# One encoder kernel with split-precision experts: which engine subtracts the low halves of the expert weights

## The reference

```python
def expert_choice_moe(h, w_router, w_gate_up, w_down):       # 16 experts, D = D_EXPERT = 1024
    aff = jax.nn.softmax((xt @ w_router).astype(jnp.float32), axis=-1)
    gate, idx = lax.top_k(aff.T, cap)                         # cap = 32 and 64 tokens: 96 for both sequences
    xs = xt[idx]
    gu = jnp.einsum('ecd,edf->ecf', xs, w_gate_up)            # 1024 x 2048 weights per expert
    g, u = gu[..., :D_EXPERT], gu[..., D_EXPERT:]
    y = jnp.einsum('ecf,efd->ecd', jax.nn.silu(g) * u, w_down) * gate[..., None]   # 1024 x 1024 per expert
    out = jnp.zeros_like(xt).at[idx.reshape(-1)].add(y.reshape(-1, D))
```

## Time and profile before

| | |
|---|---|
| three runs, median | 4184.73 us (4175.05 to 4191.94) |
| profiled execution, span from first to last instruction | 4180.8 us; its page gives no other time for it, and the span stands 3.9 us below the median of the runs |
| PE, PE weight loads | 3603.7 us (86%), 2737.9 us (65%) |
| DVE, ACT, POOL | 1949.1 us (47%), 1800.1 us (43%), 1069.5 us (26%) |
| first use of an expert's low half by PE, last scatter: layer 1 | 1395.8 us to 2087.8 us |
| last scatter, layer 2 | 4162.5 us |
| POOL low halves (L644) | 128 instructions, 612.6 us |
| DVE low halves (L1022) | 256 instructions, 878.8 us |

### The profile page before, as it was taken

One profiled execution on the slowest core, in us unless ns is written; L12 is line 12 of the kernel. 1 busy time (PEld: TensorE's weight loads), 2 busy tenths in 40 slices (PEclk: granted clock), 3 DMA queues, 4 the chain that ended last, 5 costly groups with the idle time before them and its releaser, 6 DMA issues.

```text
span 4180.8 us, 54944 instructions
## 1 busy us (share of the span) xinstructions
PE 3603.7 (86%) x19108; PEld 2737.9 (65%) x19108; DVE 1949.1 (47%) x2474; ACT 1800.1 (43%) x2780; POOL 1069.5 (26%) x604
## 2 busy tenths in 40 slices
PE   5999878899999688888869998788999987888886
PEld 4835645599998455556567375456999975556554
DVE  3423346222222777776734333452222237777775
ACT  3344445311112566666533444443111135666664
POOL 0021112100000556566500201111000005666664
PEclk9988988799999799999989899788999988999998
DMA  4101000211114689989641011002111227899896
GB/s 170 43 12 34 25 18 12 87 59 58 54 45 156 213 300 305 319 304 309 235 145 33 12 39 33 4 16 94 55 51 58 97 99 256 294 318 315 303 312 219
DMA packets 317901, 575.80 MB, mean 138 GB/s; under 512 B 14656, under 2 KB 100672, under 8 KB 317664
## 3 DMA queue, kind: packets, MB, share of 16 engines
q1 hardware_dynamic: 310288, 544.85, 37.2%
q0 software_dynamic: 7472, 29.17, 3.3%
HBM read 539.37 MB, written 40.89 MB: 139 GB/s over the span
## 4 chain that ended last, share of the span: by engine, by line
PE 70%; issue 12%; DVE 8%; POOL 6%; ACT 2%; DVEq 1%; DMA 1%; SPq 1%; POOLq 0%; ACTq 0%
PE bank L1413 13%; PE bank L1415 13%; PE bank L1414 13%; PE bank L1620 7%; PE bank L1471 5%; PE bank L1504 5%; PE bank L1641 4%; POOL wlo_more L644 4%; PE bank L1479 3%; PE bank L1499 2%; DVE wlo_more L1022 1%; PE bank L1574 1%; POOL PR L639 1%; PE bank L1576 1%; DVE YS L1400 1%
## 5 line engine op out<-in xcount | busy, mean ns | idle before, releaser
L1413 PE MATMUL bank<-whi,hT_hi 128*128 128x256 f32 (+1 forms) x2624 | 780.4, 297 | 12.3 <-DVE hT_lo L1034 6.8
L1415 PE MATMUL bank<-whi,hT_lo 128*128 128x256 f32 (+1 forms) x2624 | 743.1, 283 | 0.0
L1414 PE MATMUL bank<-wlo,hT_hi 128*128 128x256 f32 (+1 forms) x2624 | 742.9, 283 | 0.0
L639 POOL TENSOR_SCALAR PR<-PR,prec 128x256 f32<-128x256 f32 (+2 forms) x336 | 190.8, 569 | 1380.6 <-DVE prec L1190 1380.5
L1022 DVE TENSOR_TENSOR wlo<-mraw,whi 128x2048 fp32r<-128x2048 f32 x128 | 457.6, 3576 | 132.1 <-ACT whi L718 132.1
L1413 PEld LDWEIGHTS bank<-whi,hT_hi 128*128 128x128 f32 x2624 | 504.0, 192 | 20.9 <-issue 15.9
L1414 PEld LDWEIGHTS bank<-wlo,hT_hi 128*128 128x128 f32 x2624 | 504.3, 192 | 5.0
L1415 PEld LDWEIGHTS bank<-whi,hT_lo 128*128 128x128 f32 x2624 | 503.7, 192 | 0.0
L1022 DVE TENSOR_TENSOR wlo_more<-mraw,whi_more 128x2048 fp32r<-128x2048 f32 x128 | 421.2, 3290 | 99.7 <-ACT whi_more L718 99.5
L718 ACT ACTIVATE whi_more<-mraw 128x2048 fp32r<-128x2048 f32 x192 | 367.4, 1914 | 226.6 <-PE bank L1415 226.2
L718 ACT ACTIVATE whi<-mraw 128x2048 fp32r<-128x2048 f32 x192 | 366.9, 1912 | 47.2 <-PE bank L1415 47.2
(11 more groups left out here) (210 smaller groups left out, 6309.3 us busy)
## 6 DMA issues: line engine op xcount, KB each, us to landing
mraw<-in_w_gate_up_dram SPq DMA_DIRECT2D x256, 1024.0 KB, 6.1
mraw<-in_w_down_dram SPq DMA_DIRECT2D x128, 1024.0 KB, 7.1
wraw<-in_w_in_dram SPq DMA_DIRECT2D x50, 1024.0 KB, 5.4
o_rows<-OS SPq DMA_DIRECT2D x24, 384.0 KB, 2.4
oT<-o_rows SPq DMA_DIRECT2D x2, 4608.0 KB, 15.5
wdir<-in_w_branch_dram SPq DMA_DIRECT2D x8, 1024.0 KB, 7.8
wdir<-in_w_out_dram SPq DMA_DIRECT2D x8, 1024.0 KB, 5.3
xin<-x_acc SPq DMA_DIRECT2D x2, 3072.0 KB, 21.0
```

Of the source, the lines that this page charges most:

```text
L639: pool.tensor_scalar(PR[:, u % 3, 0:n], PR[:, u % 3, 0:n], prec[:, u % 4:u % 4 + 1], 1.0, ALU.mult, ALU.mult).then_inc(p_norm.sem, 1)
L1413: pe.matmul(out, lhs_hi, rhs_hi, start=first, stop=False)
L1414: pe.matmul(out, lhs_hi, rhs_lo, start=False, stop=False)
L1415: return pe.matmul(out, lhs_lo, rhs_hi, start=False, stop=last)
```

## The change

DVE makes all twelve low halves of an expert, and `lo_by_pool` with its four calls and the semaphore `lo_pool` are gone. SP and PE wait for `lo_made` where they waited for `lo_pool`. What is computed stays the same to the bit.

```diff
-POOL_EVERY = 3
-LO_PER_E = MPOS - MPOS // POOL_EVERY
...
-        lo_made = sig("lo_made", NGEMM + LO_PER_E * NE)
-        lo_pool = sig("lo_pool", (MPOS - LO_PER_E) * NE)
+        lo_made = sig("lo_made", NCHUNK)
...
# SP, both branches of m_loads (the same edit twice)
-                            if pos % POOL_EVERY == 0:
-                                sp.wait_ge(lo_pool.sem, lo_pool.at(l, e * (MPOS // POOL_EVERY) + pos // POOL_EVERY))
-                            else:
-                                sp.wait_ge(lo_made.sem, lo_made.at(l, m_lo_index(e, pos)))
+                            sp.wait_ge(lo_made.sem, lo_made.at(l, m_lo_index(e, pos)))
...
# POOL
-                lo_by_pool(l, 0, 0)
 
                 def expert(e, first, last):
-                    lo_by_pool(l, e, 3)
                     if not last:
...
-                    for pos in range(2 * POOL_EVERY, MPOS, POOL_EVERY):
-                        lo_by_pool(l, e, pos)
-                    if not last:
-                        lo_by_pool(l, e + 1, 0)
...
# DVE
-                for pos in range(1, AHEAD):
+                for pos in range(AHEAD):
                     lo_moe(l, 0, pos)
...
                         nxt = pos + AHEAD
-                        if nxt % POOL_EVERY:
-                            if nxt < MPOS:
-                                lo_moe(l, e, nxt)
-                            elif not last:
-                                lo_moe(l, e + 1, nxt - MPOS)
+                        if nxt < MPOS:
+                            lo_moe(l, e, nxt)
+                        elif not last:
+                            lo_moe(l, e + 1, nxt - MPOS)
...
# PE
-                        if pos % POOL_EVERY == 0:
-                            pe.wait_ge(lo_pool.sem, lo_pool.at(l, e * (MPOS // POOL_EVERY) + pos // POOL_EVERY))
-                        else:
-                            pe.wait_ge(lo_made.sem, lo_made.at(l, m_lo_index(e, pos)))
+                        pe.wait_ge(lo_made.sem, lo_made.at(l, m_lo_index(e, pos)))
```

More of the change, by code:

```diff
@@ L394, in m_lo_index @@
         def m_lo_index(e, pos):
-            return NGEMM + e * LO_PER_E + pos - pos // POOL_EVERY - 1
+            return NGEMM + e * MPOS + pos
         zq = Z[:, 0:2, :, :].rearrange("p c t n -> p (c t) n")
@@ L640, in norm_p @@
                                        ALU.mult, ALU.mult).then_inc(p_norm.sem, 1)
[L642 to L645, removed]
             with pool.Fori(0, DEPTH) as l:
```

## The result

| | before | after |
|---|---|---|
| median of the runs | 4181.06 us (4 runs, 4175.05 to 4191.94) | 3956.58 us (4 runs, 3954.61 to 3959.16) |
| span of the profiled execution | 4180.8 us | 3952.9 us |
| POOL busy | 1069.5 us | 375.1 us |
| DVE busy | 1949.1 us | 1932.3 us |
| PE busy | 3603.7 us | 3545.7 us |

The ratio is 0.9457, 95% interval 0.9436 to 0.9478: 5.4% faster. The forecast was 3988 us with a range of 3940 to 4070. DVE makes half as many low halves again as before and is busy for less time.

The account below looks back on a forecast made before the run. POOL's low halves, stalling PE and holding DVE, were taken as the bound. Fourteen periods cut from 43.4 to 37.0 us, plus 3.7 and 5.0 at the edges, save 98.3 us a layer, 196.6 in two: 3988 us, range 3940 to 4070.

Parts of the forecast that it names:

- The three costs of the stall: PE per expert: 4.82 us gap at position 3, 2.64 us lost to low clock behind it, 1.61 us waiting for `act_s`.
- The port: DVE's two-input subtractions and POOL's exclude each other, so POOL's 18.9 us per expert were added to DVE's.
- The walk: One expert stepped through at 2.79 us a position: no low half on DVE late in mid-loop, if data is there.
- The two places with 1 us to spare: On DVE: `act_s` of position 7 behind position 10's half (1.0 us), low part of `aT` behind position 11's (1.1 us).
- the period of 37.0 us: Expected time per expert, from a DMA need of 34.1 to 36.8 us and PE's 35.0; 43.4 before.
- the scatter's transfer: On the DMA: about 2.7 us per expert that might shut the loads out, raising the floor to 36.8 us.
- the estimate of 34.1 for loads and gather: DMA floor in us per expert without the scatter's time: (12.58 + 0.39) MB at 380 GB/s.
- the edges: Layer start to first scatter gains 3.7 us despite PE starting 1.8 later; the last expert gains 5.0.
- R1: PE alone bounds, the scatter's packets slipping between loads: period 35.5 us, 3946 us in all; chance 0.20.
- R2: DVE's queue or POOL's small steps become late: period about 39.5 us, 4063 us in all; chance 0.27.
- R3: DVE's long low halves have a cause other than POOL, so DVE bounds: about 90 us slower, 4275 us; chance 0.05.
- R4: No gain: the gap is passed on in full to DMA waits, needing a 43 us DMA floor; chance 0.03.

Follow-up runs that it names:

- g_pool_in_time: Kernel before, POOL keeping all four low halves, position 3's ahead of the scatter, the landing wait behind position 9: 4071.41 us against 4190.79, ratio 0.972.
- f_lo_first: Changed kernel with DVE's first three low halves of a layer ahead of the low parts of the first expert's tokens: median 3963.11 us.
- c_pool_reads: Changed kernel plus two POOL subtractions of an idle 128x2048 tile per expert, whose result nobody waits for: 4109.0 us, one run.

## Why the prediction was right, and where it was off

**The mechanism.** The three costs of the stall were named rightly and went: no wait of PE for a POOL half, the clock at 1.00, and PE's wait for `act_s` 0.9 us at most, none of it from POOL. The port, too, was read rightly from two rows, and two experiments show it by itself. That POOL's 18.9 us per expert were added to DVE's is too strong, though: before the change DVE's low halves took 878.8 us where 256 x 2.28 are 584, so DVE was held for 9.2 us per expert, and the rest of POOL's time fell into DVE's pauses. What the experiments add is how the 7.65 us per expert (43.4 to 35.75) divide: 4.15 are the order of POOL's queue (a version that leaves all four subtractions on POOL gets them), and 3.5 come only with the subtractions off POOL. I put these to the port, by the rows of `g_pool_in_time` and since two useless POOL subtractions alone cost 4 to 6 us a period; the 3.5 are a difference, with the transfers as the limit at their lower end, and hold what POOL's slower subtraction costs. The forecast put the gap down to position 3's place behind the scatter. That was half of it: with that place mended alone, the gap came back at position 6, and little or nothing was won.

**The low halves in time.** The walk held. In the unhindered experts PE takes 34.65 to 34.67 us; I had taken 35.0. The two places with 1 us to spare were the right ones to look at: one POOL subtraction left in the loop makes `act_s` late at just the first of them, and so do the late loads in the changed kernel.

**The step that was off: the period of 37.0 us.** It came from the DMA's floor, and the term that was mis-sized is the scatter's transfer. I let it shut out the loads for 2.7 us, from a stretch in which it ran at a share of 1.06 and 137 GB/s, and so put the floor at up to 36.8. But in that stretch no load was out. SP waited for POOL's low half, and the 67 packets of the scatter alone made up the share (waits of SP, 1655 to 1670 us, and DMA queues, 1662 to 1664 us, of the kernel before):

```profile
SPq L590 <- POOL wlo_more L644: 8.9, 1, 8.9
```

```profile
q0 software_dynamic: 67, 0.27, 105.8%
```

Such a share does not tell what loads could carry beside the scatter. With loads queued, the DMA carries all 13.37 MB at 374 GB/s in 35.75 us; without the scatter the need is 34.67 or less. So the scatter costs at least 1.1 us of a period, where 2.7 were put in the sum's upper bound, and at most 1.6, if the estimate of 34.1 for loads and gather is a floor. Over the 14 periods of a layer, three of them at 34.65, the mean is 35.51, and (37.0 - 35.51) x 14 x 2 = 42 us of the sum come from this term, with the 0.2 us put on top of the floor. The total was off by 31. In the profiled executions the two stages, each from DVE's index copy to the last scatter, gained 240.3 us against the 196.6 forecast: 42 more by this term, 3 more at the edges, and a rounding of 1 the other way. Of these 43.7 us more, 8.7 were given back ahead of layer 1's stage (below) and 4.2 between the two stages (1372.5 us before, 1376.7 after). So the range held because it had been drawn wide enough to take in R1; the likeliest sum had its largest term wrong.

**The edges.** PE starts 2.0 us later behind the low part (3.50 us of wait where it had 1.46); I had 1.8. From the low part to the first scatter the layer gained 2.5 us, not 3.7. The last expert takes 32.3 us, a gain of 7.6, not 5.0. Layer 1 in all: 120 us gained in the stage against the 98.3 forecast. Ahead of it, layer 1's stage begins 8.7 us later in the profiled execution of after; other executions of the same code vary so too (it began 12.7 us earlier with `f_lo_first`), and this part was not changed. What makes it vary was not looked into.

**The rivals.** The time fell between the forecast's own range (from 3966) and R1 (3946). R1's mechanism, PE alone, is true of the first three experts of a layer and no more; its reason, that the scatter's packets slip between the loads, is mostly right. R2 did not come: the gather had time, and POOL's copy of `ig` takes 1.4 us in the loop, 1.2 more than with DVE idle, and does not wait for several low halves. R3 and R4 are excluded.

**Open.** In the run with three halves on POOL the periods of layer 2 begin at 39 us and end at 41, with the same instructions; which order of turns at the port decides this was not tried.

## What to carry to other kernels

Before you share elementwise work between DVE and POOL, compare the longest of one DVE instruction with its shortest: if the long ones end a fixed time behind POOL's ends, as here, treat the two as one resource, and add their times. Then try it with POOL work that nobody waits for. An in-order queue that carries a stall may hide a second one behind it; mend one place and look where the wait goes before you judge the cause. And a DMA share read while nothing else is queued is no floor for a busy stage: take it from a stretch where everything competes, or give it both ends.

## What the runs showed of the hardware that I had not expected

- Waiting for the port also hits tiny instructions: POOL's copy of a 96x1 column takes 0.18 us with DVE idle, 1.40 in the changed kernel's loop, and 1.86 beside a low half at the start of a layer.
- A POOL memset of 128x2048 (1.81 us) costs DVE's subtraction nothing (2.29 us at the longest); a POOL subtraction of that size holds DVE's until it ends (5.09 and 5.69 us).
- POOL's subtractions do not always alternate with DVE's: in the kernel before one DVE half was held for 11.49 us, through two POOL subtractions in a row, while DVE got in between two of them in `g_pool_in_time` (6.07 us) and `c_pool_reads` (5.09 us). Starting first is not enough either: with three halves on POOL a DVE half started at 1661.47, beside POOL's issue of the gather, and ended at 1668.70, behind POOL's subtraction of 1661.92 to 1666.54.
- A gather of 96 rows of 4 KB beside three fresh 1 MB loads had its tokens turned 9.4 us behind the start of its issue, against 4.4 us without loads; in the first case the issue itself is 1.1 us longer.
